# Key block of a fused two-block kernel: the value products of the first two token chunks moved between key tiles

## The chip, the cores and the metric

The kernel runs on 1 core of one Trainium2 chip. The metric is the device time of one execution in microseconds (us), lower is better, taken as the median of a few runs. TensorE (PE in the profile) multiplies, VectorE (DVE) and ScalarE (ACT) work element by element, GpSimd (POOL) and SyncE (SP) here mostly issue transfers. Each engine works through its own queue of instructions in order and is tied to the others by counting semaphores: `then_inc` raises one, `wait_ge` holds the queue until the count is reached.

## The reference, cut to what matters

The reference is two transformer blocks in sequence on 512 tokens of width 1024, all in 32-bit floats. The first block runs a gated recurrence (8 heads), a sparse attention (8 query heads, 2 key and value groups) and a mixture of experts. The change lies in the sparse attention of the first block, in the projections that it reads:

```python
h = _layer_norm(x) * (1 + sc1[:, None]) + sh1[:, None]
proj = h @ w_in[l] + b_in[l]
(hq, hf, hi, hg, nq, kc, vc, ks, vs, kw, vw, ngate, mg_h, mg_n) = jnp.split(proj, split_idx, axis=-1)
...
k_cmp = _compress(to_g(kc), pos_k, w1_k, b1_k, w2_k)
v_cmp = _compress(to_g(vc), pos_v, w1_v, b1_v, w2_v)
```

`kc`, `vc`, `ks` and `kw` (two groups of 128 columns each) are wanted with features on the partitions. `vs` and `vw` (four groups of 128 columns, 512 in all) are wanted with tokens on the partitions, because they are the values that the attention weights are multiplied with.

## The kernel before, in words

`hT` holds the normalized tokens, features on partitions, 8 blocks of 128 features by 512 tokens. After the recurrence of the 8 heads the function `key_values` runs as one block of the program, in which each engine has its own written-out order. Behind it come the attention over 8 heads (`sparse_attention`), the merge of the two branches (weights sent by L1405), the output projection (L1673) and the mixture of experts (L2182 to L2238), then the second block with its own mixture.

TensorE's order in `key_values` is this. Key tiles 0 and 1 were multiplied at the end of the recurrence. `feature_major(j)` (L901) makes key tile j, for j from 2 to 7: 8 products of 128 features by 512 tokens into one of two PSUM banks; it waits for its weights in `w[j % 2]` and until ScalarE has copied tile j - 2 out of the bank. Behind each tile stands `norm.turn(pe, j - 2)` (L809), which transposes one head of the recurrence's output: 4 transposes, after ScalarE has scaled that head. Turns 6 and 7 stand behind tile 7. ScalarE scales head j right behind its copy of key tile j (L959, then L801), so turn 7 can't begin before tile 7 is done. Then come the values, `psv` (L921): for each chunk c of 128 tokens 8 products of 128 by 512, with chunk c in bank `psv[c % 2]`; chunks 2 and 3 first wait until VectorE has emptied their bank (`v_kept`). The values' weights `wv` are loaded once (L875). Behind the values come the products of the compression (L932), which need `w1` (two loads, L884), positions added by VectorE (`placed`) and the banks of the turns free; then the gate products (L907), the rest of the compression and the first queries.

A profile row of 8 products of 128x512 shows 16 matmuls: a 32-bit product is two of the trace's instructions.

VectorE's order in the same block:

```python
for group in range(4):
    rest.multiply_second(dve, group)
for h in range(HEADS):
    norm.gated(dve, h)
    if h < HEADS - 1:
        rest.multiply_second(dve, 4 + h)
dve.wait_ge(S["kept"], 8)
dve.wait_ge(ahead.pos_loaded, 16)
positions(1, second_v)
for c in range(TC):
    dve.wait_ge(S["v_projected"], c + 1)
    dve.tensor_tensor(v_tok[:, c, :], psv[c % 2][:, :], v_bias[:], ALU.add).then_inc(S["v_kept"], 1)
    if c == 0:
        positions(0, first_v)
    rest.multiply_second(dve, 3 + HEADS + c)
```

`norm.gated(dve, h)` (L814) waits for turn h and reads its bank. `rest.multiply_second` (L221) is work for a later stage: three reductions of 128x1024 on weights that GpSimd loads (L207), three slots in turn. `positions` (L984) writes the inputs of the compression; `positions(1)` writes over the buffers of the key weights. L998 is the copy of a values chunk.

SyncE's order: `wv`, the positions, key weights 4 to 7 (L879; weights j are sent when tile j - 2 is done), the first queries' weights (L427), `w1[1]`, then, when all 8 turns are done, `w1[0]` (both L884; `w1[0]` lies in `xn`, where the heads' output was), then `w2` (L885) and two tables (L1051).

Of the kernel before, what the change touches and what calls it, by code (L numbers as in the profile page):

```python
# [16 lines left out]
TC = SEQ // P  # L17
KC = D // P
HEADS = 8
# [816 lines left out]
def key_values(k, kvT, v_tok, gates, k_cmp, v_cmp, rest, ahead, gate, squares, queries, q_projected, pair, send_tables):  # L836
# [13 lines left out]
    with ExitStack() as ctx:  # L850
# [12 lines left out]
        norm = HeadNorm(k, ctx, gate, squares)  # L863
        turned_ps, = k.banks(ctx, "cmp_turned", 1)
        cmp_ps, out_k, out_v = norm.ps[0], norm.ps[1], pair[1]
        wv_loaded = k.sem(ctx, "kv_wv_loaded")
# [5 lines left out]
        with nc.Block() as block:  # L872
            @block.sync
            def _(sp):
                sp.dma_start(wv[:], w_v.rearrange("(k p) n -> p k n", p=P)).then_inc(wv_loaded, 16)  # L875
                sp.dma_start(ahead.pos[:], k.i["cmp_pos"].rearrange("s d l -> d s l")).then_inc(ahead.pos_loaded, 16)
                for j in range(4, 8):
                    sp.wait_ge(S["projected"], j - 3)
                    sp.dma_start(w[j % 2], w_kv[j]).then_inc(w_loaded[j % 2], 16)  # L879
                queries.send(sp)  # L880
                for s in (1, 0):
                    if s == 0:
                        sp.wait_ge(norm.turned, HEADS)
                    sp.dma_start(w1[s], w_cmp[s].rearrange("(l d) h -> d l h", d=P)).then_inc(w1_loaded[s], 16)  # L884
                sp.dma_start(w2[:], k.i["w_cmp2"].rearrange("s h d -> h s d")).then_inc(w2_loaded, 16)  # L885
                send_tables(sp)
# [7 lines left out]
            @block.tensor  # L894
            def _(pe):
                def feature_major(j):
                    s = j % 2
                    pe.wait_ge(w_loaded[s], j // 2 * 16 + 16)
                    pe.wait_ge(S["kept"], j - 1)
                    for kc in range(KC):  # L900
                        last = pe.matmul(ps[s][:, :], w[s][:, kc, :], k.hT[:, kc, :], start=(kc == 0), stop=(kc == KC - 1))  # L901
                    last.then_inc(S["projected"], 1)

                def gate_products(chunks):
                    for c in chunks:
                        for kc in range(KC):
                            last = pe.matmul(psg[:, c * 24:(c + 1) * 24], k.hT[:, kc, c * P:(c + 1) * P], wv[:, kc, 4 * P:NV],  # L907
                                             start=(kc == 0), stop=(kc == KC - 1))
                    return last

                for j in range(2, 8):
                    feature_major(j)
                    norm.turn(pe, j - 2)
                for h in (HEADS - 2, HEADS - 1):
                    norm.turn(pe, h)
                pe.wait_ge(wv_loaded, 16)
                for c in range(TC):
                    if c >= 2:
                        pe.wait_ge(S["v_kept"], c - 1)
                    for kc in range(KC):  # L920
                        last = pe.matmul(psv[c % 2][:, :], k.hT[:, kc, c * P:(c + 1) * P], wv[:, kc, 0:4 * P],  # L921
                                         start=(kc == 0), stop=(kc == KC - 1))
                    last.then_inc(S["v_projected"], 1)

                for s in range(2):
                    pe.wait_ge(w1_loaded[s], 16)
                pe.wait_ge(S["placed"], 4)
                pe.wait_ge(norm.bank_free, HEADS)
                for half, source in ((0, first_v), (1, second_v)):
                    for l in range(SUB):  # L930
                        for s in range(2):
                            last = pe.matmul(cmp_ps[s * 64:(s + 1) * 64, half * P:(half + 1) * P], source[s][:, :, l], w1[s][:, half * SUB + l, :],  # L932
                                             start=(l == 0), stop=(l == SUB - 1), skip_group_check=True)
                last.then_inc(S["products_done"], 1)
                gate_products(range(2))
                pe.wait_ge(S["parts_kept"], 1)
                for half in range(2):
                    last = pe.transpose(turned_ps[:, half * P:(half + 1) * P], parts[:, half * P:(half + 1) * P], k.const("ident"))
                last.then_inc(S["parts_turned"], 1)
                gate_products(range(2, TC)).then_inc(S["g_projected"], 1)  # L940
                pe.wait_ge(S["act_ready"], 1)
                pe.wait_ge(w2_loaded, 16)
                pe.wait_ge(S["kept"], 8)
                pe.matmul(out_k[:, 0:NB], w2[:, 0, :], pre[:, 0, :], start=True, stop=True)
                for g in range(GROUPS):
                    last = pe.matmul(out_v[0:N_CMP, g * P:(g + 1) * P], pre[:, 1, g * N_CMP:(g + 1) * N_CMP], w2[:, 1, :],
                                     start=True, stop=True)
                last.then_inc(S["out_done"], 1)
                pe.wait_ge(queries.loaded[0], 16)
                for kc in range(KC):  # L950
                    last = pe.matmul(pair[0][:, :], queries.w[0][:, kc, :], k.hT[:, kc, :], start=(kc == 0), stop=(kc == KC - 1))
                last.then_inc(q_projected, 1)
# [2278 lines left out]
```

## Time and profile before

| what | value |
|---|---|
| median of 3 runs | 1919.43 us (1916.26 to 1920.68) |
| the profiled execution, its own time | 1917.68 us |
| its span, first to last instruction | 1915.9 us |
| TensorE busy | 1719.5 us, 90% of the span |
| VectorE busy | 762.9 us, 40% |
| ScalarE busy | 433.1 us, 23% |
| mean granted TensorE clock | 0.956 of full |

The profile is of one execution. Its own time is 1.8 us longer than its span. Times inside the rows are counted from the span's start; the key block lies between about 315 and 425 us. An engine's busy time says how much work it has, not whether the end of the kernel waits for it; that is read from the idle times in brackets, which name what the engine waited for last. "PEclk" is the granted TensorE clock as a share of full speed, 1.00 being 2.4 GHz and 0.50 being 1.2 GHz.

### The profile page before, as it was taken

How to read it: one execution, taken by the hardware profiler on the slowest of the kernel's cores; microseconds unless marked ns; L12 is line 12 of the kernel's file. 1: busy time of each engine (PE TensorE's matmuls, PEld its weight loads, DVE VectorE, ACT ScalarE, POOL GpSimd, SP SyncE). 2: the span in 40 equal slices, each digit the busy share in tenths (PEclk: the TensorE clock that was granted, in tenths of full speed). 3: DMA queues.
4: the chain of work that ended last, by engine and by line, in shares of the span. 5: the costliest groups of instructions: out<-in, count | busy, mean ns of one | idle time of the engine just before them, and what ended most of it. 6: DMA issues, size and time to landing. Idle time of an engine off the chain costs nothing. (4 is left out here: it accounts for less than half of the span.)

```text
span 1915.9 us, 21909 instructions
## 1 busy us (share of the span) xinstructions
PE 1719.5 (90%) x8024; PEld 974.6 (51%) x8024; DVE 762.9 (40%) x1907; ACT 433.1 (23%) x1072; POOL 103.4 (5%) x127
## 2 busy tenths in 40 slices
PE   6999998999998999998988887878799999798777
PEld 3656564466667888655333332322368555533222
DVE  5544456745556655363111111111545554321115
ACT  4323232114452000022111010101222431222112
POOL 1100000000000000000000000000000000011110
PEclk9999999989999999998999898989999999899889
DMA  8643326931120622645999999999512234699995
GB/s 346 252 154 109 144 97 262 391 130 42 42 74 26 261 88 88 275 201 220 420 427 428 427 425 428 426 428 419 213 44 73 89 142 192 224 415 426 424 422 219
DMA packets 69798, 474.79 MB, mean 248 GB/s; under 512 B 11566, under 2 KB 12782, under 8 KB 45760
## 3 DMA queue, kind: packets, MB, share of 16 engines
q1 hardware_dynamic: 52944, 398.66, 51.4%
q0 software_dynamic: 15600, 70.61, 9.5%
q10 hardware_dynamic: 1152, 4.19, 0.5%
q8 instruction: 59, 0.97, 0.2%
q14 instruction: 43, 0.35, 0.1%
HBM read 459.53 MB, written 34.11 MB: 258 GB/s over the span
## 5 line engine op out<-in xcount | busy, mean ns | idle before, releaser
L2199 PE MATMUL moe_ps<-moe_up,moe_hg 128*64 128x512 f32 x1536 | 383.5, 657 | 93.6 <-DMA moe_up<-in_exp_gate 41.9
L2199 PEld LDWEIGHTS moe_ps<-moe_up,moe_hg 128*64 128x64 f32 x1536 | 131.7, 151 | 341.6 <-issue 341.3
L2238 PE MATMUL moe_ps<-moe_down,moe_midT 128*64 128x512 f32 x720 | 161.1, 596 | 14.3 <-DMA moe_down<-in_exp_down 13.8
L533 PE MATMUL mx_pair<-hT,hg_w 128*128 128x512 f32 x336 | 149.1, 596 | 1.6 <-DMA hg_w<-in_w_hg 1.6
L2291 ACT ACTIVATE moe_sig<-moe_ps 128x512 f32<-128x512 f32 (+1 forms) x32 | 15.8, 492 | 532.5 <-PE moe_ps L2199 532.5
L2320 DVE COPY moe_midT<-moe_ps 128x512 f32<-128x512 f32 (+1 forms) x32 | 17.9, 558 | 262.0 <-PE moe_ps L2210 262.0
L2330 DVE SCALAR_TENSOR_TENSOR moe_res<-moe_ps,moe_route_slot_share,moe_gain 128x512 f32<-128x512 f32 x64 | 45.1, 746 | 159.6 <-PE moe_ps L2238 159.6
L2238 PEld LDWEIGHTS moe_ps<-moe_down,moe_midT 128*64 128x64 f32 x720 | 53.8, 137 | 101.1 <-issue 98.5
L2276 ACT ACTIVATE moe_hg<-moe_ps,mod,scale_ffn 128x128 f32<-128x128 f32 x248 | 90.5, 469 | 50.8 <-PE moe_ps L2182 50.8
L533 PEld LDWEIGHTS mx_pair<-hT,hg_w 128*128 128x128 f32 x336 | 62.1, 190 | 74.2 <-issue 73.3
L2312 DVE TENSOR_TENSOR moe_mid<-moe_sig,moe_ps 128x512 f32<-128x512 f32 (+1 forms) x32 | 17.7, 555 | 162.6 <-PE moe_ps L2199 160.1
L2124 POOL DMA_INDIRECT moe_xg<-kept_rows,moe_route_slot_rows x32 | 32.4, 1014 | 524.6 <-PE moe_ps L2182 352.8
L556 PEld LDWEIGHTS mx_pair<-hg_w,hT 128*128 128x128 f32 x512 | 58.3, 192 | 4.1 <-issue 3.3
L556 PE MATMUL mx_pair<-hg_w,hT 128*128 128x128 f32 x512 | 58.6, 275 | 0.0
L1673 PE MATMUL moe_ps<-mix_out_w,mergedT 128*128 128x512 f32 x128 | 57.1, 607 | 0.0
L221 DVE CUSTOM_DVE_ANT_0 rest_w<-rest_w,onT 128x1024 f32<-128x1024 f32 x48 | 56.1, 1220 | 2.4 <-DMA rest_w<-in_mod_rest 1.5
L1673 PE MATMUL moe_ps<-mx_out_w,mx_catT 128*128 128x512 f32 x128 | 55.4, 592 | 0.0
L1179 PEld LDWEIGHTS at_o<-at_pT,at_values 128*128 128x128 f32 x320 | 43.4, 191 | 18.7 <-issue 8.6
L1134 PE MATMUL mx_pair<-hT,at_wq_w 128*128 128x512 f32 x112 | 52.5, 592 | 0.0
L901 PE MATMUL mx_pair<-hT,kv_w 128*128 128x512 f32 x96 | 44.2, 615 | 6.5 <-DMA kv_w<-in_w_kv 3.7
L1179 PE MATMUL at_o<-at_pT,at_values 128*128 128x128 f32 x320 | 47.7, 280 | 0.4 <-ACT at_pT L1232 0.4
L1424 PE MATMUL mg_ps<-hT,xn 128*128 128x256 f32 x192 | 45.4, 379 | 1.2 <-PEq L1110 1.2
(421 smaller groups left out, 2539.8 us busy)
## 6 DMA issues: line engine op xcount, KB each, us to landing
moe_down<-in_exp_down SPq DMA_DIRECT2D x44, 2048.0 KB, 34.0
moe_up<-in_exp_up SPq DMA_DIRECT2D x31, 2048.0 KB, 32.7
moe_up<-in_exp_gate SPq DMA_DIRECT2D x31, 2048.0 KB, 34.8
moe_up<-in_exp_in SPq DMA_DIRECT2D x31, 2048.0 KB, 32.9
rest_w<-in_mod_rest POOLq DMA_DIRECT2D x16, 1536.0 KB, 10.1
hg_w<-in_w_hg SPq DMA_DIRECT2D x32, 512.0 KB, 3.8
rest_w<-in_mod_rest POOLq DMA_DIRECT2D x8, 2048.0 KB, 8.6
xn<-in_w_merge SPq DMA_DIRECT2D x32, 512.0 KB, 4.4
```

The costliest lines, as they stand in the source:

```text
L221: dve.tensor_tensor_reduce(self.w[:, s, :], self.w[:, s, :], self.acts[:, 1, :], 1.0, 0.0, ALU.mult, ALU.add, self.k.mod_raw[:, at:at + 1])
L533: last = pe.matmul(proj[bank][:, :], w[s][:, kc, :], k.hT[:, kc, :], start=(kc == 0), stop=(kc == KC - 1))
L556: last = pe.matmul(proj[1][:, c * P:(c + 1) * P], k.hT[:, kc, c * P:(c + 1) * P], w[3][:, kc, :], start=(kc == 0), stop=(kc == KC - 1))
L901: last = pe.matmul(ps[s][:, :], w[s][:, kc, :], k.hT[:, kc, :], start=(kc == 0), stop=(kc == KC - 1))
L1134: last = pe.matmul(proj[:, :], wq[s][:, kc, :], k.hT[:, kc, :], start=(kc == 0), stop=(kc == KC - 1))
L1179: last = pe.matmul(o_ps[s][:, c * P:(c + 1) * P], values[:, br, kk, :], pT[u % 2][:, kk * P:(kk + 1) * P], start=(u == 0), stop=False, ski ...
L1424: last = pe.matmul(out, a[:, kc, :], b[:, kc, :], start=(first and kc == 0), stop=(kc == 3), skip_group_check=True)
L1673: last = pe.matmul(self.ps[n % 4][:, :], self.source[:, kc, c * P:(c + 1) * P], self.weights.w[h][:, kc, :], start=(kc == 0), stop=(kc == ...
L2199: last = pe.matmul(self.up_ps[u][e * SLOTS:(e + 1) * SLOTS, :], self.hg[m % 2][:, kc, e * SLOTS:(e + 1) * SLOTS], w[:, kc, :], start=(kc = ...
L2238: last = pe.matmul(self.res_ps[side][e * SLOTS:(e + 1) * SLOTS, :], self.midT[:, f, e * SLOTS:(e + 1) * SLOTS], w[e][:, f, side * 512:(sid ...
L2276: last = act.activation(self.hg[m % 2][:, kc, :], self.x_ps[kc // 4][:, kc % 4 * P:(kc % 4 + 1) * P], ACT.Identity, scale=self.scale[:, kc ...
L2330: last = dve.scalar_tensor_tensor(out=self.res[m % 2][:, cut], in0=self.res_ps[side][:, :], scalar=self.route.slot_share[:, m:m + 1], in1= ...
```

## The change

The body of the values' loop becomes a function, `token_major(c)`. Chunk 0 is now multiplied behind key tile 3 and turn 1, chunk 1 behind key tile 5 and turn 3; chunks 2 and 3 stay behind turn 7. The wait for `wv` moves along with chunk 0. Nothing is changed on the other engines: VectorE's, ScalarE's, GpSimd's and SyncE's orders and their waits are those quoted and told above.

```diff
--- before.py
+++ after.py
@@ -908,19 +908,25 @@
                                              start=(kc == 0), stop=(kc == KC - 1))
                     return last
 
-                for j in range(2, 8):
-                    feature_major(j)
-                    norm.turn(pe, j - 2)
-                for h in (HEADS - 2, HEADS - 1):
-                    norm.turn(pe, h)
-                pe.wait_ge(wv_loaded, 16)
-                for c in range(TC):
+                def token_major(c):
+                    if c == 0:
+                        pe.wait_ge(wv_loaded, 16)
                     if c >= 2:
                         pe.wait_ge(S["v_kept"], c - 1)
                     for kc in range(KC):
                         last = pe.matmul(psv[c % 2][:, :], k.hT[:, kc, c * P:(c + 1) * P], wv[:, kc, 0:4 * P],
                                          start=(kc == 0), stop=(kc == KC - 1))
                     last.then_inc(S["v_projected"], 1)
+
+                for j in range(2, 8):
+                    feature_major(j)
+                    norm.turn(pe, j - 2)
+                    if j in (3, 5):
+                        token_major(j // 2 - 1)
+                for h in (HEADS - 2, HEADS - 1):
+                    norm.turn(pe, h)
+                for c in range(2, TC):
+                    token_major(c)
 
                 for s in range(2):
                     pe.wait_ge(w1_loaded[s], 16)
```

## Rows read from the trace of the kernel before

**Rows 1.** The page: busy us, share of the span, instructions.

```profile
PE 1719.5 (90%) x8024; PEld 974.6 (51%) x8024; DVE 762.9 (40%) x1907; ACT 433.1 (23%) x1072; POOL 103.4 (5%) x127
```

**Rows 2.** Timeline of PE, key block: start us, length us, names, count, [idle <-releaser].

```profile
316.16 8.80 PE L901 MATMUL mx_pair<-hT,kv_w 128*128 128x512 f32 x16 [2.87 <-ACT at_kvT L959]
...
332.11 0.60 PE L809 MATMUL hn_ps<-consts,xn 128*128 128x128 f32 x4
332.54 7.03 PE L901 MATMUL mx_pair<-hT,kv_w 128*128 128x512 f32 x16
339.41 0.60 PE L809 MATMUL hn_ps<-consts,xn 128*128 128x128 f32 x4
342.96 7.13 PE L901 MATMUL mx_pair<-hT,kv_w 128*128 128x512 f32 x16 [2.95 <-DMA kv_w<-in_w_kv]
...
358.55 7.13 PE L901 MATMUL mx_pair<-hT,kv_w 128*128 128x512 f32 x16 [0.70 <-DMA kv_w<-in_w_kv]
365.52 1.04 PE L809 MATMUL hn_ps<-consts,xn 128*128 128x128 f32 x8
367.63 0.66 PE L809 MATMUL hn_ps<-consts,xn 128*128 128x128 f32 x4 [1.08 <-ACT xn L801]
368.12 27.63 PE L921 MATMUL kv_psv<-kv_wv,hT 128*128 128x512 f32 x64
```

**Rows 3.** Timeline of PE, the first product behind the values.

```profile
395.69 0.38 PE L932 MATMUL hn_ps<-xn,at_kvT 128*64 128x128 f32 x1
```

**Rows 4.** Timeline of DVE from turn 5 on.

```profile
366.15 0.75 DVE L814 SCALAR_TENSOR_TENSOR ohT<-hn_ps,cols,ohT 128x512 f32<-128x512 f32 x1 [4.09 <-PE hn_ps L809]
...
370.46 0.75 DVE L814 SCALAR_TENSOR_TENSOR ohT<-hn_ps,cols,ohT 128x512 f32<-128x512 f32 x1
...
374.76 0.75 DVE L814 SCALAR_TENSOR_TENSOR ohT<-hn_ps,cols,ohT 128x512 f32<-128x512 f32 x1
...
377.88 0.69 DVE L998 TENSOR_TENSOR at_v_tok<-kv_psv,value_bias 128x512 f32<-128x512 f32 x1
...
384.62 0.69 DVE L998 TENSOR_TENSOR at_v_tok<-kv_psv,value_bias 128x512 f32<-128x512 f32 x1
```

**Rows 5.** Timeline of SP: issues of transfers.

```profile
315.31 0.39 SPq L875 DMA_DIRECT2D kv_wv<-in_w_v  x1
...
324.99 25.46 SPq L879 DMA_DIRECT2D kv_w<-in_w_kv  x4
...
368.38 2.75 SPq L884 DMA_DIRECT2D xn<-in_w_cmp  x1
```

**Rows 6.** DMA issues, 300 to 420 us: KB each, us to landing.

```profile
kv_w<-in_w_kv SPq DMA_DIRECT2D x6, 512.0 KB, 8.7
kv_wv<-in_w_v SPq DMA_DIRECT2D x1, 2144.0 KB, 8.9
...
cmp_w<-in_w_cmp SPq DMA_DIRECT2D x1, 128.0 KB, 28.5
...
xn<-in_w_cmp SPq DMA_DIRECT2D x1, 0.5 KB, 21.8
```

**Rows 7.** Windows: busy us by engine, PEclk, DMA share, GB/s.

```profile
318.00:320.00 2.00, 2.00 (x3) 0.67 (x2) 1.64 (x5) 1.58 (x6) 0.00 (x0) 0.50 1.04 406
320.00:322.00 2.00, 2.00 (x5) 0.91 (x4) 2.00 (x5) 1.02 (x4) 0.00 (x0) 0.79 1.04 408
...
342.00:344.00 2.00, 1.03 (x3) 0.56 (x4) 1.03 (x3) 0.00 (x0) 0.53 (x1) 1.00 0.99 418
```

**Rows 8.** Timeline of PE in the first mixture, one wait.

```profile
1123.95 9.98 PE L2199 MATMUL moe_ps<-moe_up,moe_hg 128*64 128x512 f32 x32 [3.40 <-DMA moe_up<-in_exp_gate]
```

**Rows 9.** Timeline of PE in the second mixture, with and without a wait.

```profile
1725.98 7.04 PE L2199 MATMUL moe_ps<-moe_up,moe_hg 128*64 128x512 f32 x32
...
1743.06 9.33 PE L2199 MATMUL moe_ps<-moe_up,moe_hg 128*64 128x512 f32 x32 [5.22 <-DMA moe_up<-in_exp_in]
```

**Rows 10.** Waits of SP, 420 to 1000 us: total, times, longest.

```profile
SPq L1405 <- PE mg_ps L1424: 157.0, 14, 12.6
```

## Prediction, made before the changed kernel was run

> **What bounds the kernel now.** I read the page first: TensorE is busy for 90% of the span [rows 1], so the question for any edit in its order is which idle time it takes away or makes. Next came TensorE's timeline in the key block [rows 2]. The reader is to see three idle stretches between key tiles 2 and 7 and the values: 2.95 us before tile 5 and 0.70 us before tile 7, both ended by a load of key weights, and 1.08 us before turn 7, ended by ScalarE's scaling. The values then run as one piece of 64 matmuls, and the compression's products follow at 395.69 with no idle time in the bracket [rows 3]. So this block is bound by TensorE, less about 4.7 us of idle time, and what the block gains or loses is read at the start of those compression products. VectorE's timeline came third [rows 4]: it waited 4.09 us for turn 5 at 366.15, then it has a backlog, taking up turns 5, 6 and 7 at 366.15, 370.46 and 374.76, one every 4.31 us, because a group of reductions for a later stage stands between two of them. It copies values chunk 0 out of its bank at 377.88. That was harmless: TensorE wanted the bank for chunk 2 only at 381.9, two chunks of 6.89 us behind 368.12.
>
> **Units.** A key tile is 6.87 us from start to start and a turn 0.43 us (332.11, 332.54 and 339.41 in [rows 2]). Four values chunks take 395.69 - 368.12 = 27.57 us, 6.89 each, 13.78 for two.
>
> **Step 1, the two chunks move into the key tiles.** Nothing is added to or taken from TensorE's work, 16 matmuls a chunk as before. Chunk 0 needs `wv`, issued at 315.31 and landed 8.9 us later, 324.2, and chunk 0 starts at 332.54 [rows 5, 6]: no wait. The new order from 332.54 on: chunk 0 to 339.43, tile 4 to 346.30, turn 2 to 346.73, tile 5 to 353.60, turn 3 to 354.03, chunk 1 to 360.92, tile 6 to 367.79, turn 4 to 368.22, tile 7 to 375.09, then turn 5. Its banks are free: chunks 0 and 1 are the first users of theirs, and ScalarE and VectorE have longer between tiles than before.
>
> **Step 2, the waits for key weights go.** Weights 5 are sent when tile 3 is done, about 332.3. In the trace tile 5 began at 342.96 after a wait for them, so they had landed; now they are wanted at 346.73. Weights 6 and 7 are sent behind tiles 4 and 5, 346.5 and 353.8, and take 8.7 us by the median [rows 6], so they land by 355.2 and 362.5 and are wanted at 360.92 and 368.22. All of this idle time goes. Turn 5 comes at 375.09 and not at 365.52, 9.57 us later for 13.78 us of work put ahead of it: 4.21 us recovered. Checked from the other side: by starts the two gaps are 3.12 and 0.88 us and the two tiles behind them took 0.21 us longer than the others, 4.21 together.
>
> **Step 3, the values wait for VectorE.** Turn 7 still waits for ScalarE, which scales head 7 only behind tile 7. It ends, as before, 2.60 us behind turn 5's start (368.12 - 365.52), at 377.69. Chunk 2 comes next and needs its bank, which holds chunk 0. Chunk 0 was done at 339.4, but in VectorE's order its copy still stands behind turns 5, 6 and 7, two groups of reductions and `positions(1)`. VectorE begins this row of work at turn 5. It isn't late for it: turn 4 ends at 368.22, its gating and the group behind it take 4.31 us, so VectorE idles from 372.6 until turn 5. From there the row is that of before, shifted by 9.57 us: turns taken up at 375.72, 380.03 and 384.33, the copy of chunk 0 from 387.45 to 388.14 [rows 4]. Its loads are no later than before relative to it, as each is sent two groups ahead. Chunk 2 can't start before 388.2. TensorE idles 388.2 - 377.7 = 10.5 us. Before the change the 13.78 us of chunks 0 and 1 lay over this very row of VectorE's work; that cover is gone. Chunk 3 needs chunk 1's copy, which was at 384.62 and is at 394.2 to 394.9; chunk 2 ends at 395.1 at the earliest, so there is no second wait.
>
> **Sum without the clock.** Chunks 2 and 3 from 388.2 end at 402.0, against 395.69: +6.3 us, which is 10.5 lost less 4.2 recovered.
>
> **Step 4, the clock behind the long wait.** The trace has no idle time of 10 us in mid-kernel behind dense work, so I bound its aftermath. Behind 2.87 us of idle time tile 2 ran with 0.50 and 0.79 granted in two windows of 2 us, that is at 1.2 GHz for part of it [rows 7], and took 8.80 us and not 7.03: 1.77 us lost [rows 2]. Behind 2.95 us tile 5 kept 2.4 GHz (1.00 from 342 to 344) and lost 0.1 [rows 2, 7]. In the mixtures 32 matmuls took 9.33 us behind 5.22 us of idle time, against 7.04 behind none, 2.29 lost [rows 9], and 9.98 behind 3.40 us, 2.94 lost [rows 8]. The unknown cost lies between 0 and 2.94 us. I take 2.0, between 1.77, which is the row of the same kind of product, and 2.29, which has the idle time nearest to 10.5. The Trainium skill (TensorE: Matmul & The Clock Gate, Why this matters for your kernels) warns of idle gaps between bursts of matmuls, behind which the engine is back at the lower clock. The trace agrees only in part, since 2.87 us brought a fall and 2.95 us none; by that rule a gap of 10.5 us would surely be followed by a slow start, and the sum would be the one with a clock term and not the one of +6.3.
>
> **Step 5, what stands behind.** With the clock term chunk 3 ends at 404.0, +8.3 us. The compression needs `w1[0]`, sent when turn 7 is done: at 368.38 before, now at 378.0. It landed 21.8 us after issue [rows 5, 6], so at 399.8, hidden by 4.2 us (by 2.2 if the clock doesn't fall); the transfers around it are spaced as before. The added positions stand between the copies of chunks 0 and 1, so they are ready before 394.2. VectorE's last groups hang on the copies of chunks 2 and 3 and move with them. Behind this block the order is TensorE's: SyncE sends the merge weights when TensorE frees their place, 157.0 us of waits in 14 pieces for it [rows 10], and the mixtures' weights stand behind that in the same queue. I find no transfer that runs ahead of the block, so nothing gives the 8.3 us back.
>
> The profiled execution goes from 1917.68 to 1926.0, its span from 1915.9 to 1924.2. It lies 1.75 us under the median of the runs, so for the median I add the same 8.3: 1927.7 us.
>
> **The rivals.**
> *The clock doesn't fall.* Same wait, full speed at once, as tile 5 shows: +6.3, 1925.7. For it the one row; against it three rows with a fall, two of them behind idle times shorter than this one is.
> *`w1[0]` comes late as well.* The slowest load of the block, also into the compression's weights, took 28.5 us [rows 6]. With that, `w1[0]` would land at 406.5, 2.5 us behind the need: +10.8, 1930.2. For it: small packets and a busy transfer system; against it: the neighbours are as far apart as before, and before it took 21.8.
> *The delay is given back further on.* If a transfer-bound stage had its loads sent at times that don't move, the block's loss would vanish there, down to the 2 us or so that can't be told: 1921. For it: the mixtures do wait for weights [rows 8, 9]; against it: the queue that sends them waits for TensorE [rows 10].
> *The other side, faster.* If chunk 0's copy were done by 377.7, when turn 7 ends, only the recovery would be left: -4.2, 1915.2. The point from which it decides is 381.9: a copy done before that gives a gain, one after that a loss. For it: VectorE is idle in stretches around turns 3 to 5, so by amount of work there is room. Against it: the copy's place in VectorE's order is behind turn 7 and 388.1 follows from the order alone, 6.2 us past the point; it would take VectorE skipping most of its row.
>
> **How the numbers follow.** Forecast, 1927.7: 0.64. No fall of the clock: 0.12. Late `w1[0]`: 0.10. Given back: 0.09. Faster: 0.05. The smallest change that a measurement of this kernel tells from none is 0.2%, 3.8 us. The first three, 0.86, are slower by more than that; of "given back" 0.02 counts as slower and 0.07 as no change; of the last 0.04 as faster and 0.01 as no change. That makes 0.04 faster, 0.08 same, 0.88 slower. The range takes in the first three: from 1925.7 less the 3.2 us by which the lowest run lies under the median, 1922.5, to 1930.2 plus the 1.3 us by which the highest lies over it, 1931.5. It leaves out 0.14. The forecast's own range, by the clock term from 0.9 to 2.94, is 1926.6 to 1928.7.
>
> **What the profile after would show.** Tiles 5 and 7 without an idle bracket for weights (step 2). Turn 5 at about 375.1 and turn 7 ended at about 377.7 (steps 1, 3). A bracket of some 10.5 us before the values of chunk 2, with VectorE's copy (L998) as releaser (step 3). A granted clock of about 0.5 at the start of chunk 2 and that chunk 2 us longer (step 4). The compression's first product at about 404.0, with no wait for a load (step 5), and every later landmark, such as the first merge load and the last span, 8 us later. The prediction is wrong if the copy of chunk 0 stands earlier than 381.9, if the bracket is ended by a load, or if the mixtures begin at the old time.

## The result and the profile after

The changed kernel takes 1927.32 us (median of 5 runs, 1925.11 to 1928.98) against 1919.43 (5 runs, 1916.26 to 1920.83). The ratio is 1.0045 with a 95% interval of 1.0033 to 1.0057: slower by 0.45%, 7.9 us by the medians. The forecast was 1927.7 with a range of 1922.5 to 1931.5.

TensorE's timeline of the changed kernel in the key block, to be held against [rows 2] (L917 is now the line of the values' products):

```profile
314.69 8.61 PE L901 MATMUL mx_pair<-hT,kv_w 128*128 128x512 f32 x16 [2.87 <-ACT at_kvT L965]
...
330.44 0.60 PE L809 MATMUL hn_ps<-consts,xn 128*128 128x128 f32 x4
330.87 7.03 PE L917 MATMUL kv_psv<-kv_wv,hT 128*128 128x512 f32 x16
337.74 7.03 PE L901 MATMUL mx_pair<-hT,kv_w 128*128 128x512 f32 x16
...
345.05 7.03 PE L901 MATMUL mx_pair<-hT,kv_w 128*128 128x512 f32 x16
...
352.35 7.03 PE L917 MATMUL kv_psv<-kv_wv,hT 128*128 128x512 f32 x16
359.22 7.03 PE L901 MATMUL mx_pair<-hT,kv_w 128*128 128x512 f32 x16
...
366.52 7.03 PE L901 MATMUL mx_pair<-hT,kv_w 128*128 128x512 f32 x16
```

and the same view further on, from turn 5:

```profile
373.39 1.04 PE L809 MATMUL hn_ps<-consts,xn 128*128 128x128 f32 x8
375.50 0.66 PE L809 MATMUL hn_ps<-consts,xn 128*128 128x128 f32 x4 [1.07 <-ACT xn L801]
386.49 15.43 PE L917 MATMUL kv_psv<-kv_wv,hT 128*128 128x512 f32 x32 [10.34 <-DVE at_v_tok L1004]
401.85 0.38 PE L938 MATMUL hn_ps<-xn,at_kvT 128*64 128x128 f32 x1
```

The reader is to see three things. Tiles 5 and 7 (345.05 and 366.52) carry no bracket: the waits of 2.95 and 0.70 us for key weights are gone. A bracket of 10.34 us stands in front of chunk 2, and its releaser is the copy `at_v_tok` on VectorE. The compression begins at 401.85, 87.16 us behind the start of tile 2, where it was 395.69 - 316.16 = 79.53 us: 7.6 us more in the block. Times within the block are best taken from the start of tile 2, since the changed execution came to it 1.5 us earlier although nothing ahead of it differs (the control below shows the scatter of that).

VectorE's timeline, against [rows 4]:

```profile
374.03 0.75 DVE L814 SCALAR_TENSOR_TENSOR ohT<-hn_ps,cols,ohT 128x512 f32<-128x512 f32 x1 [3.12 <-PE hn_ps L809]
...
378.33 0.75 DVE L814 SCALAR_TENSOR_TENSOR ohT<-hn_ps,cols,ohT 128x512 f32<-128x512 f32 x1
...
382.63 0.75 DVE L814 SCALAR_TENSOR_TENSOR ohT<-hn_ps,cols,ohT 128x512 f32<-128x512 f32 x1
...
385.75 0.69 DVE L1004 TENSOR_TENSOR at_v_tok<-kv_psv,value_bias 128x512 f32<-128x512 f32 x1
```

Turns 5, 6 and 7 are taken up one every 4.30 us as before, and chunk 0, finished by TensorE at 337.7, is copied at 385.75. The row of work is the old one, moved as a whole: from turn 5 to the copy it takes 11.72 us, and 11.73 in [rows 4].

Windows of the changed kernel over the wait and behind it (columns as in [rows 7]):

```profile
380.00:384.00 4.00, 0.00 (x0) 0.00 (x0) 3.88 (x8) 0.00 (x0) 0.53 (x1) 0.50 1.11 310
384.00:388.00 4.00, 1.51 (x2) 0.83 (x3) 3.90 (x5) 0.00 (x0) 0.00 (x0) 0.50 0.99 387
388.00:390.00 2.00, 2.00 (x4) 0.81 (x3) 1.86 (x4) 0.00 (x0) 0.00 (x0) 0.65 1.05 408
390.00:392.00 2.00, 2.00 (x6) 0.88 (x5) 2.00 (x5) 0.00 (x0) 0.00 (x0) 1.00 0.96 387
```

The granted clock is at 0.50 in the wait, TensorE being idle, and is back to 1.00 only from 390 on, so that the first 3 us or so of chunk 2 run at 1.2 GHz. Chunks 2 and 3 take 401.85 - 386.49 = 15.36 us, 1.6 more than two chunks of [rows 2].

### The profile page after: what moved, and what is told of

It is laid out like the page before. It is cut to its first block and busy times, and to the rows that moved or that the text cites. A ratio compares the mean times of both kernels' runs of the same rounds, so it can differ in the third digit from the quotient of the medians.

```text
span 1924.0 us, 21909 instructions
## 1 busy us (share of the span) xinstructions
PE 1712.0 (89%) x8024; PEld 973.5 (51%) x8024; DVE 762.4 (40%) x1907; ACT 432.1 (22%) x1072; POOL 103.3 (5%) x127
## 5 line engine op out<-in xcount | busy, mean ns | idle before, releaser
L2205 PE MATMUL moe_ps<-moe_up,moe_hg 128*64 128x512 f32 x1536 | 373.1, 643 | 105.9 <-DMA moe_up<-in_exp_gate 41.2
```

Of the source, the lines that this page charges most:

```text
L2205: last = pe.matmul(self.up_ps[u][e * SLOTS:(e + 1) * SLOTS, :], self.hg[m % 2][:, kc, e * SLOTS:(e + 1) * SLOTS], w[:, kc, :], start=(kc = ...
```

## The experiments

In all of them the compared numbers are the ratio to the kernel before, taken on the same chip, and the length from the start of tile 2 to the compression's first product ("the block"): 79.5 us before, 87.2 changed. Absolute times in the expectations count from 1919.4 us for the kernel before; in these runs it took 1917.2 to 1917.8, so the ratios are what to hold them against.

**A control: the kernel before, run against itself.** No edit.

> The kernel before, unchanged, timed against itself and profiled a second time. Every theory: ratio 1.000 within 0.0015, median 1917 to 1921. It is run for two other numbers: how far a second trace of one and the same program strays, at the start of the key block (316.16 in the first trace) and at its end. If the start of the key block strays by a us or more between two traces of one program, the 1.5 us by which the changed kernel's block began earlier is scatter of the code ahead of it.

Ratio 1.0005 (0.9992 to 1.0018). The median was 1919.24 against 1917.75, and a second trace of the program has a block of 393.96 - 314.32 = 79.64 us.

```profile
314.32 8.71 PE L901 MATMUL mx_pair<-hT,kv_w 128*128 128x512 f32 x16 [3.55 <-ACT at_kvT L959]
...
340.52 8.83 PE L901 MATMUL mx_pair<-hT,kv_w 128*128 128x512 f32 x16 [2.44 <-DMA kv_w<-in_w_kv]
349.19 0.60 PE L809 MATMUL hn_ps<-consts,xn 128*128 128x128 f32 x4
```

The block began 1.84 us earlier than in the first trace and the span ended 3.1 us later (1919.0 against 1915.9). So a shift of 1.5 us at the block's start, and some us of a single span, tell nothing; the block's own length, 0.1 us apart, does. One thing was new: behind the 2.44 us wait for weights 5 tile 5 took 8.83 us, where it had taken 7.13 behind 2.95 us [rows 2]. The wait that the change removes has a clock cost in some executions and not in others. The block is as long all the same, because the wait in front of tile 5 was 0.5 us shorter and the one in front of tile 7 (0.70 us in [rows 2]) was gone.

**VectorE copies chunks 0 and 1 early.** Theory A says that the 10.3 us are VectorE's written order and nothing else.

```diff
+                def keep_chunk(c):
+                    dve.wait_ge(S["v_projected"], c + 1)
+                    dve.tensor_tensor(v_tok[:, c, :], psv[c % 2][:, :], v_bias[:], ALU.add).then_inc(S["v_kept"], 1)
                 for h in range(HEADS):
+                    if h in (2, 4):
+                        keep_chunk(h // 2 - 1)
                     norm.gated(dve, h)
...
                 for c in range(TC):
-                    dve.wait_ge(S["v_projected"], c + 1)
-                    dve.tensor_tensor(v_tok[:, c, :], psv[c % 2][:, :], v_bias[:], ALU.add).then_inc(S["v_kept"], 1)
+                    if c >= 2:
+                        keep_chunk(c)
```

> The changed kernel, with VectorE's copies of chunks 0 and 1 put in its order in front of turn 2's and turn 4's gating. Theory A (the 10.3 us wait is VectorE's written order and nothing else): the wait in front of chunk 2 is gone and chunk 3 ends some 14 us behind turn 7, about 390 on the changed kernel's scale. Then the next thing late is the load w1[0], sent at turn 7 (376.2), landed 16.7 to 21.8 us later, 393 to 398: a wait of 3 to 8 us in front of the compression. Sum against the kernel before: -4.2 recovered, plus 3 to 8, so 1918 to 1923 us. If the load were hidden as well: 1915.2. Theory B (chunk 2 is held by something else that came with the move, a bank or ScalarE): no change against the changed kernel, 1927.

Ratio 1.0014 (0.9999 to 1.0029), median 1920.21; the block is 394.49 - 313.93 = 80.56 us. TensorE's timeline, chunks 2 and 3 and the first product behind them:

```profile
375.42 13.90 PE L917 MATMUL kv_psv<-kv_wv,hT 128*128 128x512 f32 x32
```

```profile
394.49 0.48 PE L938 MATMUL hn_ps<-xn,at_kvT 128*64 128x128 f32 x1 [5.17 <-DMA xn<-in_w_cmp]
```

The wait in front of chunk 2 is gone, the two chunks take 13.9 us, and a load of 5.17 us' wait is next, inside the 3 to 8 us expected: `w1[0]`, sent at 375.67 and landed 18.8 us later. Theory B is out. It also says that the mere repair of the stall doesn't make the move pay: 4.2 us recovered went into the next wait in line.

**Chunk 0 alone moved.**

```diff
-                    if j in (3, 5):
-                        token_major(j // 2 - 1)
+                    if j == 3:
+                        token_major(0)
...
-                for c in range(2, TC):
+                for c in range(1, TC):
```

> Chunk 0 alone moved behind tile 3; chunks 1 to 3 behind turn 7. Theory A: turn 5 comes 6.89 - 3.3 = 3.6 us later than before, VectorE's copy of chunk 0 with it, done at 382.1; chunk 1 covers 371.7 to 378.6, so a wait of 3.5 us in front of chunk 2 remains. Recovered 3.3, lost 3.5, and 0 to 2 for the clock: 1919.4 to 1921.5. Rival (each chunk that is moved costs its half of the 7.9 us): 1923.4. Rival (a move by itself costs nothing until the wait passes some size): 1916.

Ratio 1.0013 (0.9999 to 1.0026), median 1919.78 against 1917.75. The block is 396.12 - 315.80 = 80.32 us.

```profile
370.24 7.03 PE L917 MATMUL kv_psv<-kv_wv,hT 128*128 128x512 f32 x16
380.75 15.44 PE L917 MATMUL kv_psv<-kv_wv,hT 128*128 128x512 f32 x32 [3.48 <-DVE at_v_tok L1004]
```

The wait is 3.48 us, 3.5 expected, ended by VectorE. And the clock fell in it, so that chunks 2 and 3 took 15.44 us (windows as in [rows 7]):

```profile
380.00:384.00 4.00, 3.25 (x4) 1.48 (x5) 3.86 (x4) 0.00 (x0) 0.00 (x0) 0.57 1.02 400
```

Both rivals named are off by the block: half of the full cost would be 83.3 us for it, and no cost 76. The ratio alone would rule out only the second, since half of the cost would be 1.0022, inside the interval. The cost isn't per chunk; it is what is left of VectorE's row once TensorE runs out of work to lay over it, 10.3 us with nothing, 3.5 with one chunk, none with two.

**The wait filled with products.** This kernel adds 11 products that the reference doesn't have.

```diff
+                for n in range(11):
+                    pe.matmul(turned_ps[:, :], wv[:, n % KC, 0:P], k.hT[:, n % KC, :], start=True, stop=True)
                 for c in range(2, TC):
                     token_major(c)
```

> The changed kernel with 11 products of 128x512 whose result nobody reads, put in front of chunk 2's wait, so that TensorE is busy for 9.5 of the 10.3 us. They add work that the reference doesn't have; the output is the same. Theory A with a clock term: chunks 2 and 3 take 13.8 us and not 15.4, the compression begins 1.6 us earlier, the time is 1925.7. Rival: the clock's fall is paid back by the next one coming later, in the gate products (the changed kernel's block behind the values was 1.8 us shorter than before's): the time stays at 1927.3.

Ratio 1.0032 (1.0019 to 1.0045), median 1923.77.

```profile
376.25 9.61 PE L929 MATMUL cmp_turned<-hT,kv_wv 128*128 128x512 f32 x22
386.76 14.00 PE L917 MATMUL kv_psv<-kv_wv,hT 128*128 128x512 f32 x32 [0.90 <-DVE at_v_tok L1006]
```

Chunks 2 and 3 took 400.69 - 386.76 = 13.93 us and not 15.36, so 1.4 us of the block were the clock's. The ratio is 0.0013 under the changed kernel's, 2.5 us, and 0.0018 under it in the repeat below; the intervals overlap, so of the kernel's time this is an indication and no more. What the rival wanted, that the clock takes its toll later if not here, isn't in the trace: from tile 2 to the first scores of the attention this kernel needs 113.4 us, the changed one 116.2.

**The changed kernel once more**, beside the next three.

> The changed kernel unchanged, on the chip of this call, so that the others stand beside it. Every theory: ratio to before 1.0033 to 1.0057; from the start of tile 2 to the compression's first product 87.2 us, within 0.5.

Ratio 1.0050 (1.0032 to 1.0069). The block is 402.00 - 314.75 = 87.25 us with a wait of 10.35, so the loss is reproduced. Its span was 1919.6 us where the first trace had 1924.0, at the same block length: a single span doesn't measure this change.

**A bank of its own for each chunk, VectorE's order untouched.**

```diff
+        value_banks = psv + [turned_ps, psg]
...
-                    if c >= 2:
-                        pe.wait_ge(S["v_kept"], c - 1)
-                        last = pe.matmul(psv[c % 2][:, :], k.hT[:, kc, c * P:(c + 1) * P], wv[:, kc, 0:4 * P],
+                        last = pe.matmul(value_banks[c][:, :], k.hT[:, kc, c * P:(c + 1) * P], wv[:, kc, 0:4 * P],
...
-                    dve.tensor_tensor(v_tok[:, c, :], psv[c % 2][:, :], v_bias[:], ALU.add).then_inc(S["v_kept"], 1)
+                    dve.tensor_tensor(v_tok[:, c, :], value_banks[c][:, :], v_bias[:], ALU.add).then_inc(S["v_kept"], 1)
...
+                pe.wait_ge(S["v_kept"], TC)
                 gate_products(range(2))
```

> The changed kernel with VectorE's order left as it is, but a PSUM bank of its own for each values chunk (chunks 2 and 3 in the banks of the compression's transposes and of the gate products, which wait for the copies). Theory A (the wait was for the bank that a late copy held): the wait in front of chunk 2 is gone and the load w1[0] ends the next one, as with the early copies: 80.5 us from tile 2 to the compression, ratio 1.001, 1920 us. Rival (VectorE's lateness holds the compression too, through the added positions): 83 us or more, ratio 1.003.

Ratio 1.0016 (1.0004 to 1.0028), median 1920.31; the block is 394.45 - 315.63 = 78.82 us.

```profile
376.64 0.65 PE L809 MATMUL hn_ps<-consts,xn 128*128 128x128 f32 x4 [1.07 <-ACT xn L801]
377.13 7.03 PE L916 MATMUL cmp_turned<-kv_wv,hT 128*128 128x512 f32 x16
384.00 7.03 PE L916 MATMUL kv_psg<-kv_wv,hT 128*128 128x512 f32 x16
```

```profile
394.45 0.48 PE L937 MATMUL hn_ps<-xn,at_kvT 128*64 128x128 f32 x1 [3.42 <-DMA xn<-in_w_cmp]
```

VectorE is as late as in the changed kernel, and TensorE doesn't care, because nothing that it needs is in the bank that waits to be emptied. With the early copies this brackets the cause: in this block VectorE's order costs TensorE time only through the one bank that it holds. The load ends the next wait here too, 3.42 us. The block is 1.7 us shorter than expected, since the load landed 17.0 us after issue. The ratio, 0.0006 above the one expected, doesn't fit the trace: by it this version's first scores come 109.4 us behind tile 2, as in the kernel before, while its median is 3.1 us longer (0.8 to 5.4 by the interval). Where those go stays open.

**Everything ahead.** The next wait in line was `w1[0]`, which is sent when the last turn is done. So the turns themselves were pulled ahead of tile 7, with ScalarE's scaling, which held turn 7.

```diff
+                turned = 0
                 for j in range(2, 8):
                     feature_major(j)
-                    norm.turn(pe, j - 2)
+                    if j < 7:
+                        norm.turn(pe, turned)
+                        turned += 1
                     if j in (3, 5):
                         token_major(j // 2 - 1)
-                for h in (HEADS - 2, HEADS - 1):
-                    norm.turn(pe, h)
+                        norm.turn(pe, turned)
+                        turned += 1
+                    if j == 6:
+                        norm.turn(pe, turned)
...
                     if j == 1:
                         norm.begin_scalar(act)
-                        norm.scale(act, 0)
-                    if j:
-                        norm.scale(act, j)
+                        for h in range(4):
+                            norm.scale(act, h)
+                    if j >= 2 and j + 2 < HEADS:
+                        norm.scale(act, j + 2)
```

VectorE's copies are those of the early-copies version, with `h in (3, 6)` and `keep_chunk(h // 3 - 1)`.

> The changed kernel with three edits around the moved chunks: ScalarE scales two heads ahead of its tile copies, the eight turns go one behind each of tiles 2 to 5 and of chunks 0 and 1 and two behind tile 6, all ahead of tile 7, and VectorE copies chunks 0 and 1 in front of the gating of turns 3 and 6. Theory A (behind the copies the load w1[0], sent at the last turn, was what was late): w1[0] is sent some 9 us earlier in the block and lands before chunk 3 ends; no wait in the block from tile 3 on. From tile 2's start to the compression 73.2 us and not 79.5 (before) or 87.2 (changed): the time is 6.3 us under before's, ratio 0.9967, faster than both. Rival (transfers, not TensorE, bound this block, so an earlier send lands no earlier): a load wait of 5 us or more again, 78 us, ratio 0.999 to 1.001.

Ratio 0.9978 (0.9964 to 0.9991), median 1913.7 against 1917.17: faster than before, and with an interval clear of the changed kernel's. The block is 388.72 - 314.57 = 74.15 us.

```profile
366.90 1.04 PE L809 MATMUL hn_ps<-consts,xn 128*128 128x128 f32 x8
367.77 7.03 PE L901 MATMUL mx_pair<-hT,kv_w 128*128 128x512 f32 x16
374.64 13.90 PE L917 MATMUL kv_psv<-kv_wv,hT 128*128 128x512 f32 x32
```

```profile
388.72 0.38 PE L943 MATMUL hn_ps<-xn,at_kvT 128*64 128x128 f32 x1 [0.19 <-DMA xn<-in_w_cmp]
```

```profile
368.02 1.61 SPq L884 DMA_DIRECT2D xn<-in_w_cmp  x1
```

From tile 3 on TensorE has no wait but 0.19 us for `w1[0]`, sent at 368.02 and landed 20.7 us later. The expectation of 73.2 us was 0.95 short: 0.19 is the load; the other 0.8 is about the time of two turns at 0.43 us, which the estimate most likely counted as idle time. By the medians the gain is 3.5 us and by the ratio 4.2, under the 5.4 us of the block. The interval, 1.7 to 6.9 us, holds all three. In the trace its lead on the mean of two traces of the kernel before is 4.6 us at the first scores and 3.5 at the first mixture, but single traces lie about 1 us apart there, so whether something is given back further on stays open. This version changes three things at once (turns, scaling and copies), and their shares weren't measured one by one.

**The turns ahead, the chunks not moved.**

```diff
                 for j in range(2, 8):
                     feature_major(j)
-                    norm.turn(pe, j - 2)
+                    if j < 7:
+                        norm.turn(pe, j - 2)
+                    if j == 6:
+                        norm.turn(pe, 5)
```

ScalarE's edit is the one just shown.

> The kernel before, all four chunks behind the tiles, with ScalarE two heads ahead and turn 5 moved behind tile 6. It says what of the version that is all ahead comes without moving the chunks. Theory A: only ScalarE's 1.1 us wait in front of turn 7 goes; the waits for key weights in front of tiles 5 and 7 stay: 78.4 us from tile 2 to the compression, ratio 0.9994, no difference that can be told. Rival (the turns were the main cost and moving chunks adds nothing): as fast as the version that is all ahead, 0.997.

Ratio 1.0013 (0.9997 to 1.0028); the block is 395.82 - 314.86 = 80.96 us, where 78.4 was expected. Two things made it longer: tile 2, from which the block is counted, and the load that the first product behind the values waited for:

```profile
314.86 10.09 PE L901 MATMUL mx_pair<-hT,kv_w 128*128 128x512 f32 x16 [3.99 <-ACT at_kvT L962]
...
342.64 7.13 PE L901 MATMUL mx_pair<-hT,kv_w 128*128 128x512 f32 x16 [2.65 <-DMA kv_w<-in_w_kv]
...
357.79 7.03 PE L901 MATMUL mx_pair<-hT,kv_w 128*128 128x512 f32 x16
...
365.53 27.63 PE L924 MATMUL kv_psv<-kv_wv,hT 128*128 128x512 f32 x64
```

```profile
395.82 0.49 PE L935 MATMUL hn_ps<-xn,at_kvT 128*64 128x128 f32 x1 [2.65 <-DMA xn<-in_w_cmp]
```

```profile
xn<-in_w_cmp SPq DMA_DIRECT2D x1, 0.5 KB, 30.0
```

ScalarE's wait is gone as expected and the one for weights 5 stays; the one in front of tile 7 isn't there, as in the control. Tile 2 took 10.09 us and not 8.80, 1.3 us that the edit has no part in. The rest of the miss is `w1[0]`: counted from the start of tile 2 it was sent at 50.9 us, 1.3 us earlier than before (52.2), but took 30.0 us to land, the longest of all runs (16.7 to 21.8 in the others). Windows of this kernel show the transfer engines busy for their whole time, a share of 1.02 to 1.04, from 355 to 375 and 1.02 from 385 to 395, as in the kernel before. Why this load fell so far back in one execution wasn't tested and stays open. In this trace, then, an earlier send didn't bring an earlier landing, as the rival of the version with everything ahead had it. What the run does settle is that the turns alone don't give the gain of that version; their intervals don't meet. That version moved the chunks as well.

All of them together, in us from the start of tile 2:

| version | compression begins | first scores | ratio to before |
|---|---|---|---|
| everything ahead | 74.15 | 105.04 | 0.9978 |
| before (two traces) | 79.53, 79.64 | 110.36, 108.85 | 1.0005 against itself |
| four banks | 78.82 | 109.43 | 1.0016 |
| chunk 0 alone | 80.32 | 111.27 | 1.0013 |
| early copies | 80.56 | 111.84 | 1.0014 |
| turns ahead, chunks not moved | 80.96 | 111.65 | 1.0013 |
| wait filled | 85.94 | 113.41 | 1.0032 |
| changed (two traces) | 87.16, 87.25 | 116.23, 116.46 | 1.0045, 1.0050 |

All lengths hold tile 2 itself, which took 8.61 to 8.80 us in nine traces and 10.09 in that of "turns ahead".

## Why the prediction was right

**Steps 1 and 2, the recovery.** Expected: both waits for key weights gone, turn 5 9.57 us later, 4.21 us recovered. Measured from the start of tile 2, turn 5 came at 58.70 us (373.39 - 314.69) against 49.36 (365.52 - 316.16): 9.34 us later for two chunks. The 0.2 us of difference is tile 2 itself, 8.61 and not 8.80 us. Right.

**Step 3, the stall.** Expected 10.5 us, ended by VectorE's copy; measured 10.34, and 10.35 in the repeat, with `at_v_tok` as releaser. By starts, as the expectation had reckoned it, from turn 5 to the next values chunk are 13.10 us (386.49 - 373.39) and not 2.60: 10.5 exactly. The cause is shown from three sides: copied early, the wait is gone; with other banks it is gone with VectorE as late as ever; with one chunk left as cover it is 3.48 us.

**Step 4, the clock.** Expected 2.0 us within 0 to 2.94; measured 1.6 by the length of chunks 2 and 3 and 1.4 by the filled wait. The mechanism was right, the size 0.4 to 0.6 too high. The row of the same kind of product, 1.77, was nearer than the mixtures', but that is partly luck: tile 2 of the version with the turns ahead, the same product again, lost 3.06 us behind 3.99 us of idle time, above the highest bound of the prediction. One count in the prediction is wrong: of its three rows with a fall all three, not two, stand behind idle times shorter than 10.5 us, which made its case against the rival stronger than it said. The windows give it once more: from 386.49 to 388 at 0.50 and from 388 to 390 at 0.65, chunk 2 loses 0.76 + 0.70 = 1.5 us. The Trainium skill (TensorE: Matmul & The Clock Gate, Terms) reckons the penalty as the time at the lower clock times the share of pulses held back, which is this sum, and the trace agrees: 1.5 us by it, 1.6 and 1.4 measured.

**Step 5, what stands behind.** No load waits in the changed kernel: `w1[0]` was sent at 376.24 and landed 16.7 us later, at 392.9, 9 us ahead of its use. The expectation took 21.8 us for it. Nothing gave the loss back. The first merge weights went out at 555.16 and not 550.83, which with the 1.5 us of earlier start is 5.8 us, and 6.7 as a mean of two traces each. The first product of the first mixture came later too (before, then changed):

```profile
891.78 7.09 PE L2199 MATMUL moe_ps<-moe_up,moe_hg 128*64 128x512 f32 x32 [0.43 <-ACT moe_hg L2276]
```

```profile
895.78 8.16 PE L2205 MATMUL moe_ps<-moe_up,moe_hg 128*64 128x512 f32 x32
```

Behind tile 2 that is 575.6 and 581.1 us (574.5 in the control, 581.0 in the repeat), 6.0 us by the means. The medians ended 7.9 us apart. One thing on the way wasn't foreseen. Between the compression and the first scores the changed kernel made up 1.8 us:

```profile
409.44 3.75 PE L907 MATMUL kv_psg<-kv_wv,hT 128*128 128x24 f32 x32
...
413.29 6.85 PE L907 MATMUL kv_psg<-kv_wv,hT 128*128 128x24 f32 x32
...
421.55 8.10 PE L957 MATMUL mx_pair<-hT,at_wq_w 128*128 128x512 f32 x16
430.92 0.49 PE L1154 MATMUL mx_pair<-at_kvT,at_q 128*128 128x128 f32 x2 [1.28 <-ACT at_q L1217]
```

The first gate products took 3.75 us where before they took 4.49, and the first queries 8.10 and not 8.81: the fall to the lower clock came at another point of this stretch. It comes here while TensorE is busy without a break. In the changed kernel's windows:

```profile
410.00:414.00 4.00, 4.00 (x36) 4.00 (x35) 0.44 (x4) 0.48 (x2) 0.00 (x0) 0.91 0.00 0
414.00:418.00 4.00, 4.00 (x20) 4.00 (x21) 0.64 (x3) 1.63 (x3) 0.00 (x0) 0.50 0.00 0
```

In the control the same program before took 3.75 as well, and its first scores came 108.85 us behind tile 2, against 110.36 in the first trace. From the compression to the first scores it needed 29.2 us, as the changed kernel did (29.1 and 29.2), and 30.8 in its first trace. So two traces of one program differ here by 1.6 us, and the 1.8 us can't be put down to the change. Averaged over two traces each, the first scores come 116.3 us behind tile 2 with the change and 109.6 without: 6.7 us.

**The sum.** Forecast +8.3 us, made of +10.5, -4.2 and +2.0; the block gave +7.6, of +10.5, -4.2, +1.6 and -0.2 for tile 2, rounded one by one. That the medians (7.9 us, and 7.3 in the repeat) agree so closely with the sum is partly luck, as single executions of one program lie some us apart.

**The rivals.** That the clock doesn't fall: no, in both traces of the changed kernel it was at 0.50 in the wait and behind it, and with the wait filled chunks 2 and 3 were 1.4 us shorter. That `w1[0]` is late as well: not here, but it was the next thing in line, and showed as soon as the stall was taken away. That the delay is given back: not seen at the merge weights, the first mixture or the end. The other side, faster: its condition was a copy done before 381.9, and the version with early copies makes it true; it still didn't gain, because that rival hadn't priced the load behind it (it needed the load by about 391.5 and had it sent at 378).

## What to carry to other kernels

Work moved out of a stretch may have been the cover of another engine's work: ask what the moved instructions lay over, and walk that engine's written order to the point where the moved result is consumed. Here the consumer's order was left as it was, so chunk 0 sat in its bank for 48 us after the product was done (337.7 to 385.75), and 4 us of recovered idle time were paid for with 10. When a stall is repaired, look at once for the next wait in line (here a load tied to the last turn): of all versions only the one in which the chunks, their copies, the turns and with them that load were all ahead was faster, at a ratio of 0.9978.

## What the runs showed of the hardware

The clock behind short waits isn't decided by the wait's length alone: tile 5 kept 2.4 GHz behind 2.95 and 2.65 us and lost 1.8 us behind 2.44, in three executions of nearly the same order. Tile 2, whose wait is 2.87 to 3.99 us, ran at 1.2 GHz for a part of its time in every trace, but didn't always begin so. In the first trace of the kernel before it began at 316.16 at full clock and the fall came while it ran:

```profile
316.00:318.00 2.00, 1.84 (x4) 1.01 (x5) 0.00 (x0) 1.97 (x4) 0.00 (x0) 0.86 0.74 160
```

with 0.50 in the window behind it [rows 7]. So a product that starts at 1.00 may still pay for the wait in front of it. Chunk 2 began at 0.50 behind 3.48 and 10.34 us.

For 128x512 products a fall cost 1.6 to 1.8 us in tile 2 of nine traces, in tile 5 of the control and in chunk 2, and the longest wait no more than the short ones. Once, in tile 2 of the version with the turns ahead (10.09 us against 7.03), it cost 3.06.

The load of `w1[0]`, the same in all versions, took from 16.7 to 30.0 us to land. Counted from the start of tile 2, it was sent once at 50.9 us and took 30.0; at 52.2 to 54.7 it took 20.2 to 21.8 (four traces); at 61.6 to 61.8 it took 16.7 to 18.8 (five traces). Around the late sends the transfer engines had room, a share of 0.61 from 376 to 378 in the changed kernel, and around the early ones none, 1.05 from 365 to 375 in the kernel before. That this is why is argued from the shares and not tested; the 30.0 us stand on one trace.
